# Attention scores of the gated linear layer: only the keys up to each block's end

## The reference

```
bcum = jnp.cumsum(lg, axis=3)                     # within a chunk of 32 tokens
q_dec = q * jnp.exp(bcum)
k_intra = k * jnp.exp(-bcum)
k_state = k * jnp.exp(blast - bcum)
att = jnp.where(causal, jnp.einsum('nbhid,nbhjd->nbhij', q_dec, k_intra), 0.0)
o_intra = jnp.einsum('nbhij,nbhje->nbhie', att, v)
o_inter = q_dec @ s ;  s = exp(blast) * s + k_state.T @ v     # from chunk to chunk
```

## Time and profile before

| | |
|---|---|
| median of three runs | 1655.56 us (1652.19 to 1656.39) |
| profiled execution, first to last instruction | 1651.1 us |
| TensorE matmul busy | 1613.4 us, 98% of the span |
| TensorE weight load busy | 1501.1 us, 91% |
| VectorE busy | 818.7 us, 50% |
| ScalarE busy | 458.2 us, 28% |
| GpSimd busy | 375.8 us, 23% |
| mean granted TensorE clock | 0.990 |

### The profile page before, as it was taken

One profiled execution on the slowest core, in us unless ns is written; L12 is line 12 of the kernel. 1 busy time (PEld: TensorE's weight loads), 2 busy tenths in 40 slices (PEclk: granted clock), 3 DMA queues, 4 the chain that ended last, 5 costly groups with the idle time before them and its releaser, 6 DMA issues.

```text
span 1651.1 us, 25118 instructions
## 1 busy us (share of the span) xinstructions
PE 1613.4 (98%) x9827; PEld 1501.1 (91%) x9827; DVE 818.7 (50%) x1271; ACT 458.2 (28%) x969; POOL 375.8 (23%) x384
## 2 busy tenths in 40 slices
PE   6999999999999999998999999999999999999996
PEld 5899999999999999998788898888998989979896
DVE  4654449443944475457224562245622356224475
ACT  4321112111211121123325413154040541315423
POOL 3022212211211212211314223133130322314310
PEclk8999999999999999998999999999999999999998
DMA  9512221221122121210202212022120221201312
GB/s 330 193 56 87 62 63 42 84 74 42 55 78 64 57 67 54 77 41 27 64 18 73 84 40 77 13 64 84 53 66 12 64 96 40 77 13 40 110 37 108
DMA packets 137545, 115.03 MB, mean 70 GB/s; under 512 B 6013, under 2 KB 120281, under 8 KB 137442
## 3 DMA queue, kind: packets, MB, share of 16 engines
q1 hardware_dynamic: 135616, 112.87, 22.0%
q10 hardware_dynamic: 1834, 0.74, 0.2%
HBM read 99.05 MB, written 15.00 MB: 69 GB/s over the span
## 4 chain that ended last, share of the span: by engine, by line
PE 94%; DVE 3%; SPq 1%; DMA 1%; ACT 1%; issue 0%; ACTq 0%; DVEq 0%
PE psA L549 40%; PE psB L549 29%; PE psB L1804 8%; PE psA L1804 4%; PE psB L1860 2%; PE psB L1877 2%; PE psX L1842 2%; PE psB L1868 2%; PE psX L1897 1%; DVE a_hi L637 1%; PE psB L1909 1%; PE psX L1720 1%; DMA ada<-in_ada_w 1%; DVE y_rows L1606 0%; PE psB L1910 0%; PE psX L1661 0%
## 5 line engine op out<-in xcount | busy, mean ns | idle before, releaser
L344 POOL TENSOR_TENSOR w_lo<-stage,w_hi 128x1024 fp32r<-128x1024 f32 x100 | 249.7, 2496 | 891.1 <-ACT w_hi L339 891.1
L339 ACT ACTIVATE w_hi<-stage 128x1024 fp32r<-128x1024 f32 x100 | 107.0, 1070 | 433.7 <-PE psB L549 297.6
L549 PE MATMUL psA<-h_hi,w_hi 128*128 128x362 f32 (+1 forms) x864 | 210.9, 349 | 4.1 <-DVE h_lo L453 3.8
L549 PE MATMUL psA<-h_lo,w_hi 128*128 128x362 f32 (+1 forms) x864 | 193.6, 329 | 0.0
L549 PE MATMUL psA<-h_hi,w_lo 128*128 128x362 f32 (+1 forms) x864 | 193.1, 329 | 0.0
L549 PEld LDWEIGHTS psA<-h_hi,w_hi 128*128 128x128 f32 x864 | 151.4, 190 | 27.1 <-issue 21.2
L549 PEld LDWEIGHTS psA<-h_hi,w_lo 128*128 128x128 f32 x864 | 151.5, 190 | 0.0
L549 PEld LDWEIGHTS psA<-h_lo,w_hi 128*128 128x128 f32 x864 | 151.4, 190 | 0.0
L549 PE MATMUL psA<-a_hi,w_hi 128*128 128x362 f32 (+1 forms) x480 | 109.7, 334 | 2.6 <-DVE a_lo L640 1.9
L549 PE MATMUL psB<-h_hi,w_hi 128*128 128x362 f32 (+1 forms) x480 | 109.7, 331 | 0.0
L549 PE MATMUL psB<-h_hi,w_lo 128*128 128x362 f32 (+1 forms) x480 | 107.9, 327 | 0.0
(11 more groups left out here) (345 smaller groups left out, 2790.6 us busy)
## 6 DMA issues: line engine op xcount, KB each, us to landing
stage<-in_gla_w_in SPq DMA_DIRECT2D x40, 512.0 KB, 3.8
stage<-in_pool_w_in SPq DMA_DIRECT2D x32, 512.0 KB, 4.1
ada_stage<-in_ada_w SPq DMA_DIRECT2D x24, 512.0 KB, 3.8
ada<-in_ada_w SPq DMA_DIRECT2D x16, 512.0 KB, 8.4
stage<-in_pool_w_out SPq DMA_DIRECT2D x16, 512.0 KB, 3.4
v<-in_state_gla SPq DMA_DIRECT2D x32, 256.0 KB, 2.6
out_new_gla_sample<-v SPq DMA_DIRECT2D x32, 256.0 KB, 2.1
stage<-in_gla_w_out SPq DMA_DIRECT2D x16, 512.0 KB, 3.7
```

What stands on the lines that cost most here:

```text
L339: nc.scalar.activation(slot_hi(plan, j), stage[:, j % 2, :], ACT.Copy).then_inc(lay.hi_done, 1)
L344: nc.gpsimd.tensor_tensor(slot_lo(plan, j), stage[:, j % 2, :], slot_hi(plan, j).bitcast(f32), ALU.subtract).then_inc(lay.lo_done, 1)
L549: last = nc.tensor.matmul(ps[u][:, t, 0:width], weight(w[:, p, :], k), a[:, k, n0:n0 + width], start=(k == 0 and pas == 0), stop=(k == kt ...
```

## The change

`scores(s)` takes as stationary operand only the keys up to the block's own end: 32, 64, 96 and 128 columns for the blocks 0 to 3, and writes only the partitions of these keys. Partitions behind them keep what was in PSUM; they lie outside the causal mask, and `att_out` doesn't copy them. With that the zeros in `Kp` are read by nobody, and the memset on GpSimd, its semaphore and ScalarE's wait for it are gone.

```
-        kp_zero, kp_exp, kp_ready = sem("kp_zero"), sem("kp_exp"), sem("kp_ready")
+        kp_exp, kp_ready = sem("kp_exp"), sem("kp_ready")
...
                 wait_apart(pool, L1.unit_done, units(GP, g, GP.unit["LG"] + 1))
-                pool.memset(Kp[:], 0.0).then_inc(kp_zero, 1)
...
                 nc.scalar.activation(ks_s[:], ks_s[:], ACT.Exp).then_inc(smp_exp, 1)
-                act.wait_ge(kp_zero, g + 1)
...
                     for b in range(4):
-                        last = nc.tensor.matmul(X[0][:, b * CH:(b + 1) * CH], Kp[:, b, :], qd[:, b * CH:(b + 1) * CH],
-                                                start=True, stop=True)
+                        keys = slice(0, (b + 1) * CH)
+                        last = nc.tensor.matmul(X[0][keys, b * CH:(b + 1) * CH], Kp[:, b, keys],
+                                                qd[:, b * CH:(b + 1) * CH], start=True, stop=True)
                     last.then_inc(att_done, 1)
```

## The result

| | before | after |
|---|---|---|
| median of 20 runs | 1654.93 us (1651.61 to 1657.06) | 1657.71 us (1655.03 to 1660.03) |
| ratio to before | | 1.0019 (95% interval 1.0012 to 1.0026) |
| profiled execution, first to last instruction | 1651.1 us | 1657.9 us |
| GpSimd instructions | 384 | 380 |

The change makes the kernel slower by 0.19%. Of 1655 us that is 3.1 us (2.0 to 4.3); the forecast was 3.4 more. Its absolute figure, 1659.0 us, lies 1.3 above the median measured, and 0.6 of that is the starting point: three runs of the kernel before had given 1655.56, twenty gave 1654.93. The difference lies under the 0.3% that I had set as the bound for telling one; with 20 runs of each, it can be told.

The account below looks back on a forecast made before the run. TensorE was taken to bound the kernel: per superchunk, 0.26 us gained from shorter loads against 0.36 for three width changes, 0.105 more, times 32 is 3.4 us; 1655.56 + 3.4 = 1659.0 us, range 1654.5 to 1663.5.

Parts of the forecast that it names:

- What bounds the kernel: Scores' stretch of a head: TensorE busy 53.00 of 53.00 us, so a microsecond in its sequence is one of the kernel.
- Part 1, shorter loads: Scores' weight loads: shorter with fewer columns, 0.26 us less per superchunk, 8.2 us in all if nothing else counted.
- Part 2, the emptying: Scores: array emptied at three float32 width changes per superchunk, costing 0.36 us against the loads' gain of 0.26.
- the way from 32 to 64: Between blocks 0 and 1: load 0.028, stream 0.027, emptying 0.097, together 0.15 us; no such change in the earlier trace.
- the slow rival: Both inner width changes: emptying fixed at 0.20 behind the last matmul's start, 7.3 us more, 1662.9 us; chance 20%.
- the sum: Whole kernel: 3.4 us more, profiled span 1651.1 to 1654.5, median 1655.56 to 1659.0 us.
- 96 columns count as 128 do: Block 2 to block 3: 96 float32 columns share the width class of 128, like 79, so no emptying between them.
- Part 3, the memset: GpSimd's 0.52 us memset and ScalarE's wait: removing both is worth nothing; 2.1 us if the cover were gone.
- The supply of `Kp`: Third superchunk's first load: `Kp` ready 0.08 us ahead; longer scores ask for it later, cost taken as nothing.
- the rival of 28 late rounds: `Kp` supply becomes late, 0.1 us in each of 28 rounds, 2.8 us more, 1661.8 us; chance 3%.
- The last sign: Whole kernel: an end over 1 us off the forecast, with gaps as forecast, means something besides the scores' sequence moved.

Follow-up runs that it names:

- the run with 64, 64: Kernel before with 64, 64, 96 and 128 stationary columns in the scores, memset kept: ratio 1.0010 to before.
- the one with the changed order: Changed kernel with the blocks issued 0, 2, 1, 3 (32, 96, 64, 128 columns): 1661.58 us, ratio 1.0042 to before.
- tiles of 32: Changed kernel with each block's keys cut into groups of 32, 20 pairs per superchunk instead of 8: 1645.75 us, ratio 0.9951 to before.
- the order by key groups: Same 20 pairs of 32 keys, issued by key group (four matmuls onto partitions 0 to 31 first, then three, two, one): ratio 0.9950 to before.

## Why the prediction was right

| start, us behind the last fill matmul | forecast | trace after, mean of 32 |
|---|---|---|
| block 0, first load | 0.254 | 0.253 |
| block 0, second | 0.282 | 0.282 |
| block 1, first | 0.432 | 0.432 |
| block 1, second | 0.487 | 0.487 |
| block 2, first | 0.665 | 0.664 |
| block 2, second | 0.748 | 0.745 |
| block 3, first | 0.831 | 0.828 |
| block 3, second (D) | 0.943 | 0.939 |

- What bounds the kernel: right. The stretch has no idle time of TensorE, and what D says arrives in the time: 32 x 0.105 = 3.4 us, against 3.1 (2.0 to 4.3).
- Part 1, shorter loads: right, and shown by itself at 66 columns, D 0.636 where 0.61 was expected (0.63 in the 28 superchunks without a wait).
- Part 2, the emptying: right in place, number and size. Its riskiest step was the way from 32 to 64, taken from line 1932, whose matmul moves one column; the run with 64, 64 and the one with the changed order confirmed it. The Trainium skill's rule in "TensorEngine Tiling (Array Packing)", Key Properties, that a change of mode drains TensorE while a change of tile doesn't, agrees with these runs: one change more costs 0.118 us per superchunk, and twenty pairs within one class, on four column groups, start 0.011 us apart. The steps of 0.150 and 0.178 were measured as 0.150 and 0.177. So the slow rival, a fixed 0.20 behind the last matmul, is out: the 64-column load starts 0.124 behind the last 32-column matmul's start, where the way out of line 1720 has 0.20. What is waited for is the end of the stream, here 32 moving columns, there 128. The prediction had argued against that rival with 0.14 behind line 1932's second matmul; it took 0.207 for that matmul's record, a median over both shapes. The second 64-column record is 0.197 long, which makes it 0.125 and the argument stronger; no term of the sum hangs on it.
- The description of the kernel before and the prediction name four lines with few stationary columns, but there are more. `sample_inter` (L1897, float32, 32 columns, 512 moving) is one that stands among the scores' superchunks: TensorE changes class on the way in and out 16 times. The load behind it starts 0.52 us behind its last matmul's start, which is the 0.43 of 512 moving columns and 0.09, the same rule as above. No run here changes that line. Line 1804 (fp32r, 64 columns among 128) changes without such a wait, as fp32r did in the scores.
- That 96 columns count as 128 do, from 79 columns of a transpose: right.
- Part 3, the memset: right, shown by the run with the memset kept.
- The supply of `Kp`: right that the changed kernel doesn't meet it. Only the third superchunk of each head has the slack of 0.08; the others have 1.39 or more, so the rival of 28 late rounds could only have been one of four. In the changed kernel it has grown to 0.45. It does come as soon as the scores get shorter: with tiles of 32, the idle ahead of 4 of 32 first loads ends with GpSimd. The 1.0 us in the view is the whole idle; these loads start at 0.277 to 0.281 instead of 0.254, so the supply itself costs 0.1 us in all. With fp32r operands, where no emptying hides it, it is 1.4 and 2.2 us of idle. In the view of that line, what ended the idle of its loads with the tiles:

```profile
  issue: 6.3, 28
  POOL Kp L965: 1.0, 4
```

- Off was one remark. I wrote that the weight-load time falls by about 11 us. The sum of the records falls by that (64 each of 192, 161, 134 and 107 ns instead of 256 of 191: 38 against 49). The page's busy time counts overlapping records once, and fell by 3.8.
- The last sign, an end more than 1 us away from the sum, did come: the profiled span is 1657.9 and not 1654.5. It doesn't speak against the mechanism. Of the 6.8 us between the two profiled executions 3.4 lie in the scores, and 3.35 came about ahead of the first head's value product. The sign was too sharp for one execution of each kernel.
- The chances: I gave 0.63 to less than 0.3% and 0.29 to slower; the truth, 0.19% slower, lies where the sum had it.

## What to carry to other kernels

Fewer stationary columns shorten a weight load, by 0.87 ns a column here, but in float32, changing between 32, 64 and more than 64 columns from one product to the next costs about 0.1 us for the emptying and takes the head start of the next load. (Measured were 32, 64, 66, 79, 96 and 128 columns; whether 65 is above the boundary, and what fewer than 32 or 33 to 63 do, was not.) Before narrowing one product in a dense stream, look at the loads of any product of that type that is already narrow: an idle of 0.23 us ahead of it, ended by nothing, is a first sign. The mark alone isn't enough. In the trace of before, a 128-column load has it too, behind 512 moving columns:

```profile
1090.14 1.02 PE L1877 MATMUL psB<-v,ksT 128*128 128x512 f32 x2
...
1090.57 0.19 PEld L549 LDWEIGHTS psA<-h_hi,w_hi 128*128 128x128 f32 x1 [0.24 <-issue]
```

That load starts together with the second of the two matmuls (1090.14 + 1.02 - 0.59 = 1090.57), so its head start is intact. A load that pays for a change starts behind the stream of the matmul ahead. Either stay above the boundary (66 columns instead of 32 and 64 won 7 us where 32 and 64 lost 3), or put a whole run of products into one class, on alternating column groups, so that two changes are shared by many.

## What the hardware showed that was not expected

- Twenty float32 load and matmul pairs of 32 columns, on four column groups, start within 0.22 us, about 0.011 us a pair, where eight pairs of 128 columns take 0.84.
- Loads of another column group start while an earlier load in program order is held by its own group (the groups are inferred, as said there): with the order by key groups D rose by 0.113 us, where strict order would have given 0.31.
- fp32r products of 32, 64 and 96 columns ran among 128-column ones with no idle ahead of their loads but the waits for GpSimd's `Kp` (2.2 us in all).
